# Another order of the second layer's mixer steps on all engines, and one GpSimd step exchanged in the first layer

## What is computed

```python
for l in range(2):
    a = rms_norm(h, attn_norm[l])
    proj = a @ w_in[l]                       # columns for three head groups
    # DSA: 4 query heads, one key/value head, an indexer that picks 128 keys per query
    dq, dk = rope(rms_norm(dq)), rope(rms_norm(dk)); iq, ik = rope(iq), rope(ik)
    score = sum_h iw[h] * relu(iq[h] @ ik.T / 8) / 2
    o_a = softmax(dq @ dk.T / 8 on the top_k(score, 128) keys) @ dv
    # FoX: 4 heads, forgetting gate as a bias of cumulated log-sigmoids
    o_b = softmax(rms_norm(fq) @ rms_norm(fk).T / 8 + c_q - c_k) @ fv
    # GLA: 4 heads, gated linear attention in chunks with a carried state
    o_c = rms_norm(gla(gq, gk, gv, log_sigmoid(glr @ w2 + b) / 16)) * silu(gg)
    h = h + concat(o_a, o_b, o_c) @ w_out[l]
    f = rms_norm(h, ffn_norm[l])
    h = h + (silu(f @ w_gate) * (f @ w_up)) @ w_down[l]
```

## Time and profile before

| | |
|---|---|
| median of the runs | 1249.81 us |
| the profiled execution's own time | 1249.35 us |
| its span, first to last instruction | 1247.6 us |
| granted TensorE clock, mean | 1.000 |
| TensorE busy | 1234.7 us, 99% |
| VectorE busy | 1022.6 us, 82% |
| ScalarE busy | 700.8 us, 56% |
| GpSimd busy | 169.9 us, 14% |
| the chain that ended last | TensorE 92%, issue 3%, VectorE 2%, GpSimd 2%, ScalarE 1% |

### The profile page before, as it was taken

The page is one execution under the profiler, slowest core; times in us unless marked ns, Lnnn a source line. Parts: engine busy times, 40 slices in busy tenths (PEclk is TensorE's granted clock), DMA queues, the critical chain, the costliest instruction groups (busy, mean ns, idle before and its releaser), DMA issues.

```text
span 1247.6 us, 23727 instructions
## 1 busy us (share of the span) xinstructions
PE 1234.7 (99%) x9344; PEld 1182.6 (95%) x9344; DVE 1022.6 (82%) x1692; ACT 700.8 (56%) x1158; POOL 169.9 (14%) x120
## 2 busy tenths in 40 slices
PE   7999999999999999999999999999999999999999
PEld 7999999999999999999998999888899999998998
DVE  5777789588999999897664888895989999989865
ACT  6666547656555555753355765385665555558332
POOL 2564213100000000000033463031000000000000
PEclk9999999999999999999999999999999999999999
DMA  5322111132322222233323222010322332212333
GB/s 199 97 73 86 52 35 35 35 135 73 131 102 102 102 102 69 84 102 113 108 87 98 89 71 86 18 51 18 135 102 102 128 110 102 102 69 85 118 119 119
DMA packets 27131, 113.74 MB, mean 91 GB/s; under 512 B 3344, under 2 KB 3984, under 8 KB 21648
## 3 DMA queue, kind: packets, MB, share of 16 engines
q1 hardware_dynamic: 26304, 111.18, 26.5%
q10 hardware_dynamic: 720, 1.09, 0.2%
HBM read 108.79 MB, written 2.10 MB: 89 GB/s over the span
## 4 chain that ended last, share of the span: by engine, by line
PE 92%; issue 3%; DVE 2%; POOL 2%; ACT 1%; DMA 0%; POOLq 0%; SPq 0%; ACTq 0%; DVEq 0%
PE ps L1387 22%; PE ps L1393 11%; PE ps L1002 11%; PE ps L1104 6%; PE ps L1098 6%; PE ps L1099 6%; PE ps L1008 5%; PE ps L1471 5%; PE ps L1507 4%; PE ps L1476 2%; PE ps L1512 2%; PE ps L1228 2%; PE ps L1176 1%; PE ps L1211 1%; PE ps L1201 1%
## 5 line engine op out<-in xcount | busy, mean ns | idle before, releaser
L1098 PE MATMUL ps<-xhi,whi 128*128 128x264 f32 (+1 forms) x616 | 174.5, 311 | 0.0
L1099 PE MATMUL ps<-xlo,whi 128*128 128x264 f32 (+1 forms) x616 | 167.6, 300 | 0.0
L882 POOL TENSOR_TENSOR wlo<-raw,whi 128x1024 fp32r<-128x1024 f32 x48 | 117.0, 2440 | 181.1 <-ACT whi L1685 180.7
L1098 PEld LDWEIGHTS ps<-xhi,whi 128*128 128x128 f32 x616 | 116.1, 188 | 4.5 <-issue 0.4
L1099 PEld LDWEIGHTS ps<-xlo,whi 128*128 128x128 f32 x616 | 116.2, 189 | 3.6
L1685 ACT ACTIVATE whi<-raw 128x1024 fp32r<-128x1024 f32 x74 | 78.0, 1054 | 48.5 <-PE ps L1008 30.3
L1104 PE MATMUL ps<-xhi,wlo 128*128 128x264 f32 (+1 forms) x616 | 100.4, 305 | 0.0
L1104 PEld LDWEIGHTS ps<-xhi,wlo 128*128 128x128 f32 x616 | 85.3, 188 | 4.1
L1387 PE MATMUL ps<-fhi,hi_a 128*128 128x264 f32 (+1 forms) x352 | 88.2, 283 | 0.0
L1387 PE MATMUL ps<-flo,hi_a 128*128 128x264 f32 (+1 forms) x352 | 88.1, 282 | 0.0
L1387 PE MATMUL ps<-flo,hi_b 128*128 128x264 f32 (+1 forms) x320 | 80.3, 283 | 0.0
(11 more groups left out here) (373 smaller groups left out, 3852.5 us busy)
## 6 DMA issues: line engine op xcount, KB each, us to landing
raw<-in_weights SPq DMA_DIRECT2D x116, 512.0 KB, 3.5
raw<-in_groups SPq DMA_DIRECT2D x42, 1024.0 KB, 4.8
out_hT<-h SPq DMA_DIRECT2D x7, 256.0 KB, 4.5
h<-in_hT SPq DMA_DIRECT2D x4, 264.0 KB, 6.1
h<-in_hT ACTq DMA_DIRECT2D x4, 264.0 KB, 5.9
cst<-in_consts SPq DMA_DIRECT2D x1, 780.5 KB, 9.3
xnb<-feat SPq DMA_DIRECT2D x10, 66.5 KB, 2.0
feat<-xnb SPq DMA_DIRECT2D x10, 66.5 KB, 2.2
```

The costliest lines, as they stand in the source:

```text
L882: nc.gpsimd.tensor_tensor(wlo[:, b], raw[:, b], whi[:, b].bitcast(F32), ALU.subtract).then_inc(split_done, 1)
L1098: nc.tensor.matmul(o, whi[:, k % 2, n], xhi[:, n, cut], start=(n == 0), stop=False)
L1099: nc.tensor.matmul(o, whi[:, k % 2, n], xlo[:, n, cut], start=False, stop=False)
```

## The change

Three things:

1. In the second layer all five order strings are new: 168 of 288 TensorE steps, 124 of 186 of ScalarE's, 136 of 204 of VectorE's, 11 of 38 of GpSimd's and 6 of 31 on SP's queue stand at another place. The jobs that take PSUM banks keep their order among themselves, so each has the bank that it had. The two `rope` products keep their place among these jobs.
2. In the first layer one pair on GpSimd changes places: the remainder of tile 8 now stands ahead of `clear_even`.
3. GpSimd counts its remainders (`halved`) and, ahead of each clearing step, waits until the last of them is done (`squares_halved`).

```diff
@@ layer 0 @@
-     POOLE: "AAQAQAAACACAQAAQCACAAQAAAQAAAACACCCAAA",
+     POOLE: "AAQAQAAACACAQAACQACAAQAAAQAAAACACCCAAA",
@@ layer 1, two of the five strings @@
-     POOLE: "QQAAAAAAACACCAAQQACAQAAAAAQAAACAACCAAC",
-     DMAE: "AEEEAAGAEAEAGAAAAAAAAAAAAAAAAAA"},
+     POOLE: "QQAAAAAAACACACACQQAAQAAAAQAAAACACCAAAC",
+     DMAE: "AEEAEAGAAEEAAGAAAAAAAAAAAAAAAAA"},
...
-                split, zeroed = [2 + l * UNITS], [0]
+                split, zeroed, halved = [2 + l * UNITS], [0], [0]
...
+                def squares_halved():
+                    if halved[0]:
+                        pool.wait_ge(ev.sq_split, halved[0])
...
                 def clear_even():
                     pool.wait_ge(split_done, 2 + split[0])
+                    squares_halved()
                     pool.wait_ge(ev.parted, 2)
...
                 def square(k):
...
                     nc.gpsimd.tensor_tensor(sq_parts[:, 0], sqb[:, 0], sq_parts[:, 1].bitcast(F32), ALU.subtract).then_inc(ev.sq_split, 1)
+                    halved[0] += 1
```

More of the change, by code:

```diff
@@ L266 @@
      "XXAcAXXeUAXUXUVXVVXcVWWWWece",
-     POOLE: "AAQAQAAACACAQAAQCACAAQAAAQAAAACACCCAAA",
+     POOLE: "AAQAQAAACACAQAACQACAAQAAAQAAAACACCCAAA",
      DMAE: "AEEEAGAAEAEAGAAAAAAAAAAAAAAAAAA"},
-    {PE: "AAAAAAAAABDAAAAAAAFAAAAALAADAMMAMADAMMMAAAFMAMADMAAAAMADAAAAADAXAAAXAAXAAAYYXAMAMAaAMAADAMAALLAXAPAA"
-     "PZAAYAAZAYAAXAAAXAZYXAAAaZYXbALZYXZAYXAAAZAYAXZbAYAAXAMaARARLAMPAAAPALALASTSRATRASTSdRATZYXTZYXZYAXZ"
-     "YbXdDAadZZYAYXADXZAYZbXYXZYXaZAYXZDZAYYXdbXZYXZaZYYdXZbXYdZXYaZXYZXZYXYbDZYZYZaZdbfdffff",
-     ACTE: "BCADAAAIHCLIADIMMHPMCIADMMMACMAMDMCIMADCIIJDXIAOCXAYYJXMXaJAMMDAJMLLPAXPPYAXYYXXAAaYLXYXYPKYAXYXMAaX"
-     "LMPPLALTTTUeTYAYXXTCYYXeACDaeXYUYDAXYCXYXXUaYXYXDCYYUXYeXaYYeXXYXeaYXVAYVXXYVXYDYYVaee",
-     DVEE: "AADAAAFAAIHIDIAMMHMIDMMAMFMNAMDNAADIIAAXIDAIXNNXOXANMMMNNANMNNDNAPNNAAXNNNNANANPNNPXAAXPXPAXAcNXNXNP"
-     "NANAXMMNMXARARNNAMNNNANNNSNSRNNNRSANcRSeNNXXNAXNXceNNNXNNeDUXDcXXANNXXUNNADXcXUXUeXecXeXVVVXWXWXcWDV"
-     "Wece",
-     POOLE: "QQAAAAAAACACCAAQQACAQAAAAAQAAACAACCAAC",
-     DMAE: "AEEEAAGAEAEAGAAAAAAAAAAAAAAAAAA"},
+    {PE: "AAAAAAAAABADAAAAAAFAAAAAALADMAMAAMDAMAMMAFMMAADAAAAAAMMADAAADAAXAAXAAAXYYAAXAAAMMAaMAADMALALAXAPAPAA"
+     "ZAYZAAYXXAAAZAYXAAAAAAaZAAYXbAAALZAYXAZAYXZAYXZbYXAMaAARRAAALAMAPAPAALLASTSRAATRSTSdRATZYXTZYXZYXZYb"
+     "XdADaAdZZAYYXADXAZYZbXYAXZYXaZYXZDZAYAYXdbXZYXZaZYYdXZbXYdZXYaZXYZXZYXYbDZYZYZaZdbfdffff",
+     ACTE: "BACADAAIHICALDMIMHCIMADAMMMCMMADCOAMICMDJIAIDXIXYCYPXJAMXAaMMDMAJLJLPAPPYXAYXYXXAaYPXLKAYXYXYXYMaALM"
+     "PAPXALLTTTeTAXYYTCYXYeXUXDCeaYYAXUDAYCXYXaYXYUXDCXYYUXYeXaYYeXXVeYXaAYXYVXXYVYXDYYVaee",
+     DVEE: "AADAAAFIAAIHDMIAMHMIDMMAMFMANMDNAADINIAANIXDXIXOXAMANMMNNAAMNNDNNPXNNNANNNANNANXAXPXAPNAAPPcXAPNAXNX"
+     "NXAMNMMXNANRRNNMANANANNNSNNSRNRNSNRSecNXNANXNXXNecNNNAXeNNDDXcUXXAXNNXNUNDAXcXUXUeVXecXeVXWXVXXcWDVW"
+     "Wcee",
+     POOLE: "QQAAAAAAACACACACQQAAQAAAAQAAAACACCAAAC",
+     DMAE: "AEEAEAGAAEEAAGAAAAAAAAAAAAAAAAA"},
 )
```

## The result

The changed kernel took 1254.81 us (median of 6 runs, 1253.35 to 1255.27), the kernel before 1249.78 in the same comparison (6 runs, 1248.95 to 1250.64): ratio 1.0039, 95% interval 1.0029 to 1.0049. It is slower by 5 us. The prediction said 1248.3. The profiled execution of the change took 1255.27 us, its span is 1253.5, its mean granted clock 0.999.

What follows compares the result with a forecast made beforehand. TensorE was taken as the bound, VectorE nearly a second one late in the second mixer. Gains of -1.85, taken as -2.0 for understated stalls, plus 0.5 gave -1.5 us: 1248.3 us, range 1246.9 to 1251.1.

Steps and rivals of the forecast that it cites:

- Layer 0, -0.45: First layer, tile 8: GpSimd's remainder ahead of clear_even starts near 83.5 us and ends TensorE's wait, -0.45 us.
- Tile 5, -0.3: Second layer: gate_split moved down lets ScalarE's square come earlier, ending the norm product's 0.32 us wait, -0.3 us.
- Tile 7, -0.7: Second layer: VectorE's eviction ahead of lowest(1) ends TensorE's 0.69 us wait at the norm product, -0.7 us.
- Tile 19, -0.4: Second layer, block 4: ScalarE's earlier weight rounding ends TensorE's 0.39 us wait for GpSimd's remainder, -0.4 us.
- New waits, +0.5: Second layer's new order: waits the earlier trace cannot show, bounded by 0 and 2.1 us, taken as 0.5.
- three places: Tile 8's norm product, block 1's FoX logits (meeting part(9)) and turn_tile(19): at most 0.7 us new wait each.
- With as many collisions as before: Second layer: GpSimd subtractions hold VectorE products up by up to 2.14 us each; their number was assumed unchanged.
- Rival C: Two more GpSimd collisions on the squares' path delay tile 8's norm product: +2.4 us, 1252.3 us, chance 0.10.
- the marks: Signs of error: TensorE's waits from 690 to 800 us over 1 us, or three or more 2.6 us index products.

Runs made afterwards that it cites:

- e1: Changed kernel with the second layer's five order strings put back, first layer's exchange and counted waits kept: 1248.94 us, ratio 0.9997.
- e8: Old second-layer order, first layer as changed, with gate_split later and unit 7's eviction and proj(23)'s rounding earlier: 1251.43 us.
- e12: Old second-layer order, first layer as changed, proj(23)'s rounding earlier and that step's GpSimd subtraction cut to an eighth: 1248.73 us.
- e2: Changed kernel with both evictions of unit 8 moved ahead of select(1) on VectorE: 1254.02 us.
- e14: Changed kernel with part(8) moved up behind meta_turn(0,1) and part(9) behind proj(12)'s rounding on ScalarE, second layer: 1253.59 us.
- e15: Changed kernel with GpSimd's subtractions of units 7 to 10 each cut into four instructions, nothing left out: 1250.17 us.
- e4: Changed kernel with norm(0), the squares and SP's packs at the second mixer's start back in the old order: 1253.84 us.
- e7: e4 with one more move on TensorE, logits(1,1,0) behind proj(13,1,2): 1253.81 us.
- e11: Old second-layer order, first layer as changed, with only proj(23)'s rounding moved up on ScalarE: 1251.55 us.

## Why the prediction was wrong, point by point

**Layer 0, -0.45: right in size.** GpSimd's remainder started at 84.19, not 83.5, since the subtraction ahead of it ran until then; the wait is gone, and e1 is 0.5 us faster, though its interval does not exclude nothing.

```profile
84.19 1.80 POOL L976 TENSOR_TENSOR sq_parts<-sqb,sq_parts 128x532 fp32r<-128x532 f32 x1
...
88.16 0.66 PE L1130 MATMUL ps<-sq_parts,ones_r 128*128 128x266 f32 x4
```

**Tile 5, -0.3: right in the mechanism,** and worth more: piece 2 is 0.56 us shorter in the change and 0.58 in e8, for a wait of 0.32.

**Tile 7, -0.7: the wait went, the time did not.** In e8 piece 3 is 41.47 against 41.50: what TensorE won at tile 7 it lost at unit 9, 0.7 us, where VectorE's evictions had no slack.

**Tile 19, -0.4: wrong.** The product came 0.45 us sooner behind the step ahead of it, meta_values(0,4), and the next step, values(1,4,0), only 0.1 sooner: 1.46 us behind meta_values(0,4) in the change and in e12, 1.56 before and in e1. The values' bank must first be read by VectorE's scale(0,4), which ends at 856.29 before and 861.62 after, and the norm product's wait lay beside that one. So the wait that the list put down to GpSimd cost 0.1 us, not 0.39. Before, then after:

```profile
854.94 0.60 PE L1243 MATMUL ps<-v_meta,p_meta_t 128*128 128x260 f32 x2
856.50 1.00 PE L1228 MATMUL ps<-v_fox,probs_t 128*128 128x65 f32 x8
...
855.87 0.42 DVE L2427 TENSOR_TENSOR o_tok<-ps,stat 128x256 f32<-128x256 f32 x1
```

```profile
860.27 0.60 PE L1254 MATMUL ps<-v_meta,p_meta_t 128*128 128x260 f32 x2
860.81 0.76 PE L1130 MATMUL ps<-sq_parts,ones_r 128*128 128x266 f32 x4
861.73 1.08 PE L1239 MATMUL ps<-v_fox,probs_t 128*128 128x65 f32 x8 [0.16 <-issue]
...
861.20 0.42 DVE L2438 TENSOR_TENSOR o_tok<-ps,stat 128x256 f32<-128x256 f32 x1
```

**New waits, +0.5: this is the step that failed.** In its place stand 6.1 us by the medians (5.0 lost in all, with 0.5 won in layer 0 and 0.56 in piece 2), or 5.75 by the pieces (1.16, 3.45, 1.11 and 0.03). The waits themselves are 4.1 of it (2.49, 0.95 and 0.56). I bounded them by three places with the longest wait then in the list, 0.7 us each. A wait in the list is no bound for one that does not exist yet. And of the three places one was hit as named (part(9), 0.8 us); the start was not among them (1.2 us, a pack that went behind a weight load on SP), and neither was unit 9, because I looked for slack at makers on ScalarE and read VectorE's share of busy time, not its gaps. Between 691.7 and 705.3 it had none of over 0.1 us before the change.

**"With as many collisions as before": the same step's other half.** The price of up to 2.14 us per collision was right as an upper end: of the six after, three cost 2.02 to 2.14 and three about 1.0. The count was set to no change without following the moved subtractions against VectorE's list, where two more instructions met one ahead of unit 9's bank. Rival C named this mechanism, with 1252.3 us and a chance of 0.10, and put TensorE's wait at tile 8's norm product, one of the places where it appears once unit 9's is taken away (e2, e14). Its sum had two collisions but no second place and no lost start.

**Of the marks,** TensorE's waits between 690 and 800 sum to over 3 us, which was to prove me wrong and did. The count of index products of 2.6 us was too narrow a mark: norms, rope rows, splits and select were held up as well.

## What to carry to other kernels

Read an engine's gaps, not its share: where one works back to back for 10 us ahead of something the bound engine needs, its slack can be nil even with no wait listed (0.06 us here), and with two more meetings with GpSimd that stretch took 3.45 us more. Before moving the steps of one of two engines that hold each other up, lay both lists side by side in time, and count the meetings; if they can't be kept apart, cut the long instruction in pieces, which here brought back 4.5 us of 5.0 (e15). A wait that is gone counts only when the next step starts sooner. On a DMA queue a small transfer that the bound engine needs soon belongs ahead of a large load: behind one, the last pack of rope rows took 3.7 us to land instead of 2.0.

## What the runs showed of the hardware

**Which instructions are held up.** In both profiles VectorE's MAX8, MATCH_REPLACE8 and evictions from PSUM run at their usual time beside GpSimd's subtractions, and the index product between them does not. From the change:

```profile
727.37 0.77 DVE L2245 TENSOR_TENSOR feat<-ps,rstd 128x264 f32<-128x264 f32 x2
728.06 2.14 DVE L2364 SCALAR_TENSOR_TENSOR score<-relu,w_idx,score 128x400 f32<-128x400 f32 x1
730.23 0.44 DVE L2375 MAX8 top<-score 128x8 f32<-128x272 f32 x1
...
727.37 5.10 POOL L882 TENSOR_TENSOR wlo<-raw,whi 128x1024 fp32r<-128x1024 f32 x2
```

MATCH_REPLACE8 is the same in both (0.43 us for 128x272 beside a subtraction and elsewhere). The hold does not depend on the size of VectorE's instruction in e2, where one of 128x1 elements took 2.4 us. The Trainium skill, page "SBUF — State Buffer", section "SBUF: two separate sides", says that the port pair goes to whichever instruction starts first, for its whole length, and that of VectorE's this concerns those with two SBUF inputs or in a two-port mode. These rows, e2 and e15 agree.

**The half clock.** It followed TensorE's idle times of 2.49 (the change), 2.46 (e4) and 2.5 us (e7), and one of 1.89 (e11); it did not follow 2.50 (e14), 2.18 (e4) or 1.88 (e8). So the idle time ahead does not tell it in these profiles. Ahead of unit 10 it cost nothing in the end: e14 ran at full clock, waited 0.89 us at tile 8's norm product instead, and took 45.03 us for piece 3 like the kernels with the half clock (44.97, 45.35, 45.03). In block 4, where nothing behind it was late, it cost e11 1.6 us in piece 5 against e8, with the same wait ahead:

```profile
853.00:854.00 1.00, 1.00 (x6) 0.87 (x4) 0.68 (x2) 0.34 (x1) 0.00 (x0) 0.64 0.95 393
854.00:855.00 1.00, 1.00 (x7) 1.00 (x7) 1.00 (x3) 0.43 (x2) 0.00 (x0) 0.50 0.13 49
```
